# A two-phase encoder layer: the second phase turns its operands through memory and on VectorE, with three tiles in flight

## The reference

```python
h = rmsnorm(x, norm_g) * (1 + scale) + shift
rq, rk, rv, rg, aq, ak, av, ag = split(h @ w_in)           # 3328 columns
r_out = head_norm(retention(rope(rq), rope(rk), rv)) * silu(rg)    # 4 heads of 128
a_out = softmax_with_sink(aq @ ak.T / 8, window) @ av * silu(ag)   # 8 query heads, 2 key heads of 64
y = concat([r_out, a_out]) @ w_out
x = x + gate * y;   out = rmsnorm(x, final_g)
```

## Time and profile before

| what | value |
|---|---|
| median of 3 runs | 1991.48 us (1989.26 to 1991.83) |
| the profiled execution | 1995.48 us, span 1993.7 us |
| TensorE busy | 1938.5 us (97%), clock 0.989 of full |
| VectorE, ScalarE, GpSimd busy | 1089.7, 634.3, 150.9 us |
| second phase, 927 to 1993.7 us | TensorE busy 1041.31 us, VectorE 563.41, ScalarE 405.92, transfers 90 GB/s |

### The profile page before, as it was taken

The page is one execution under the profiler, slowest core; times in us unless marked ns, Lnnn a source line. Parts: engine busy times, 40 slices in busy tenths (PEclk is TensorE's granted clock), DMA queues, the critical chain, the costliest instruction groups (busy, mean ns, idle before and its releaser), DMA issues.

```text
span 1993.7 us, 30575 instructions
## 1 busy us (share of the span) xinstructions
PE 1938.5 (97%) x10240; PEld 1596.4 (80%) x10240; DVE 1089.7 (55%) x2507; ACT 634.3 (32%) x1537; POOL 150.9 (8%) x340
## 2 busy tenths in 40 slices
PE   4999999999999999998899999999999999999997
PEld 2778888888888888887688888888888888888885
DVE  3645555555555555566455555545555554555554
ACT  2312222222222221233334333333434334343332
POOL 0000000000000000000000000000000000000000
PEclk8999999999999999999899999999999999999999
DMA  9654444444444444436424243332424333242431
GB/s 350 206 142 118 117 111 115 108 110 120 120 120 120 110 111 116 108 99 184 127 69 116 63 110 82 92 105 68 116 68 105 88 86 106 67 116 70 104 79 35
DMA packets 460480, 222.22 MB, mean 111 GB/s; under 512 B 405016, under 2 KB 412376, under 8 KB 459424
## 3 DMA queue, kind: packets, MB, share of 16 engines
q1 hardware_dynamic: 460448, 221.81, 40.8%
HBM read 137.33 MB, written 84.42 MB: 111 GB/s over the span
## 4 chain that ended last, share of the span: by engine, by line
PE 91%; issue 3%; DMA 2%; DVE 2%; SPq 1%; ACT 0%; POOL 0%; POOLq 0%; DVEq 0%; ACTq 0%
PE bank L1140 74%; PE bank L1331 3%; PE bank L1314 3%; PE bank L1302 2%; PE bank L1303 2%; PE bank L1272 1%; PE bank L1213 1%; PE bank L1214 1%; PE bank L1218 1%; DMA fin_g<-in_final_g 1%; PE bank L1390 1%; PE bank L1261 1%; DMA xn_scratch<-xn 1%; SPq L386 0%; PE bank L1415 0%
## 5 line engine op out<-in xcount | busy, mean ns | idle before, releaser
L1140 PE MATMUL bank<-wh,hh 128*128 128x512 f32 x1584 | 407.3, 399 | 7.6 <-ACT wh L311 4.4
L1140 PE MATMUL bank<-wl,hh 128*128 128x512 f32 x1584 | 397.4, 393 | 0.0
L1140 PE MATMUL bank<-wh,hl 128*128 128x512 f32 x1584 | 397.2, 393 | 0.0
L1140 PEld LDWEIGHTS bank<-wl,hh 128*128 128x128 f32 x1584 | 294.9, 188 | 74.0 <-issue 12.3
L1140 PEld LDWEIGHTS bank<-wh,hl 128*128 128x128 f32 x1584 | 295.7, 188 | 62.0
L1140 PEld LDWEIGHTS bank<-wh,hh 128*128 128x128 f32 x1584 | 291.2, 190 | 65.9 <-ACT wh L311 4.7
L646 ACT ACTIVATE hf<-xn,tiny_a 128x128 f32<-128x128 f32 (+1 forms) x248 | 98.6, 480 | 383.3 <-DVE xn L817 383.3
L709 ACT ACTIVATE s_row<-s_row,tiny_b 128x256 f32<-128x256 f32 x264 | 131.1, 498 | 151.0 <-DVE tiny_b L1001 151.0
L1140 PE MATMUL bank<-wh,yh 128*128 128x512 f32 x528 | 149.7, 405 | 2.2 <-DVE yl L1085 2.2
L1140 PE MATMUL bank<-wh,yl 128*128 128x512 f32 x528 | 146.1, 399 | 0.0
L1140 PE MATMUL bank<-wl,yh 128*128 128x512 f32 x528 | 143.5, 394 | 0.0
(11 more groups left out here) (151 smaller groups left out, 2532.2 us busy)
## 6 DMA issues: line engine op xcount, KB each, us to landing
xt<-in_x_prompt SPq DMA_DIRECT2D x64, 512.0 KB, 3.9
h_scratch<-hf SPq DMA_DIRECT2D x33, 512.0 KB, 2.9
hf<-h_scratch SPq DMA_DIRECT2D x33, 512.0 KB, 4.5
out<-xt SPq DMA_DIRECT2D x32, 512.0 KB, 2.9
xn_scratch<-xn SPq DMA_DIRECT2D x31, 512.0 KB, 2.9
xp<-xn_scratch SPq DMA_DIRECT2D x124, 128.0 KB, 3.5
aq_scratch<-aq_row SPq DMA_DIRECT2D x31, 512.0 KB, 3.5
aq_row<-aq_scratch SPq DMA_DIRECT2D x124, 128.0 KB, 3.6
```

What stands on the lines that cost most here:

```text
L1140: ins = mm(out, a[:, k, :], b[:, k, :], start=first and n == part[0] and k == chunks[0], stop=last and n == part[-1] and k == chunks[-1])
```

## The change

TensorE transposes nothing in the second phase. What is turned goes out to DRAM with `store_blocks` (four stores, 32 partitions each), comes back with one plain load, and VectorE transposes its 32 x 32 blocks: queries and keys together (`aqk_row`, 640 wide), the probabilities of each half (`p_in`, 1024 wide), the gate (512 wide). A slot now holds the front of tile t, the middle of t - 1 (scores, softmax, weighing) and the back of t - 2 (output product, residual sum); the final norm and the store of y are those of t - 3. The scores are three passes (high x high, high x low, low x high) of heads of 64 rows, two key heads side by side on the row halves of the array, with `tile_position`. The masks, banks and semaphores follow; the copies of k on GpSimd fall away, since the two halves of `ak_h` are used in turn. Retention and attention chunks of the output product are done together. The other edits (the sample tile's cached keys, the mask table's order, tile 0) follow from these.

```diff
+            def store_blocks(dst, src, stored):
+                for i in range(4):
+                    sp.dma_start(dst.rearrange("(b r) (i n) -> r b i n", r=32, i=4)[:, :, i, :],
+                                 src[32 * i:32 * (i + 1)]).then_inc(stored, 16)
             def slot_b(i, u):            # SP
...
                     wait(sp, b_split, t + 1)
                     sp.dma_start(hf[:, :, :].rearrange("p k r -> p (k r)"), h_dram[t + 1]).then_inc(hb_loaded, 16)
+                    wait(sp, fin_done, t - 2)
+                        sp.dma_start(y_prompt[bass.ts(t - 3, P), :], xts[1 - u][:, :]).then_inc(y_stored[1 - u], 16)
+                    wait(sp, yr_turned, t - 1)
+                    load_blocks(yr_in, yr_dram[t - 1], yr_loaded)
+                    for half in range(2):
+                        wait(sp, exp_done, 2 * (t - 1) + half + 1)
+                        store_blocks(p_dram[2 * (t - 1) + half], s_row[:, half], p_stored[half])
+                    wait(sp, y_stored[1 - u], 16 * (i - 1 + u))
+                        sp.dma_start(xts[1 - u][:, :], x_prompt[bass.ts(t - 1, P), :]).then_inc(xb_loaded[1 - u], 16)
+                    wait(sp, p_stored[0], 4 * 16 * t)
+                    sp.dma_start(p_in[:, 0].rearrange("p b n -> p (b n)"), p_dram[2 * (t - 1)]).then_inc(p_loaded[0], 16)
+                    wait(sp, gate_scaled, t)
+                    store_blocks(g_dram[t - 1], a_gates[1 - u][:, :].rearrange("p (b n) -> p b n", b=4), g_stored)
+                    wait(sp, kv_done, t + 1)
+                    wait(sp, aq_done, t + 1)
+                    store_blocks(aqk_dram[t], aqk_row, aqk_stored)
+                    wait(sp, p_stored[1], 4 * 16 * t)
+                    sp.dma_start(p_in[:, 1].rearrange("p b n -> p (b n)"), p_dram[2 * (t - 1) + 1]).then_inc(p_loaded[1], 16)
+                    wait(sp, g_stored, 4 * 16 * t)
+                    sp.dma_start(a_gates[1 - u][:, :], g_dram[t - 1]).then_inc(g_loaded, 16)
+                    wait(sp, aqk_stored, 4 * 16 * (t + 1))
+                    sp.dma_start(aqk_row[:, :, :].rearrange("p b n -> p (b n)"), aqk_dram[t]).then_inc(aqk_loaded, 16)
...
             def slot_b(i, u):            # ScalarE
+                    # sums of squares of t - 3
+                    # yh[:, 4:8] <- g_t (ya)
                     softmax(*prev, 0)
+                    kv_rows_out()
                     softmax(*prev, 1)
+                        aq_rows_out()
+                    # gate: two tanh, then the high part of the next h
+                    # aq_h, ak_h <- aqk_f
...
+            def turn_p(i, u, half):      # VectorE
+                t = 2 * i + u
+                wait(dve, p_loaded[half], 16 * (t + 1))
+                V.transpose(s_row[:, half].rearrange("p b n -> p (b n)"),
+                            p_in[:, half].rearrange("p b n -> p (b n)")).then_inc(pt_done, 1)
             def slot_b(i, u):            # VectorE
+                    wait(dve, pv_ready, 2 * (t - 1))
+                    wait(dve, gate_turned, t - 1)
+                    V.tensor_tensor(ya, qv_b[:, :].rearrange("p (j i r) -> p j i r", j=4, i=4), ya, ALU.mult).then_inc(ya_done, 1)
                     mask_max(*prev, 0)
+                    mask_max(*prev, 1)
+                    # yl[:, 4:8] <- ya - yh
+                    wait(dve, frstd_done, t - 2)
+                    V.scalar_tensor_tensor(xts[1 - u][:, :], xts[1 - u][:, :], rstd, fin_g[:, :], ALU.mult, ALU.mult).then_inc(fin_done, 1)
+                    split_yr(i - 1, u)
+                    # den, rden; four operations, gate_scaled
+                    turn_p(*prev, 0)
+                    # ag: four operations, ag_done
+                    turn_p(*prev, 1)
+                    wait(dve, g_loaded, 16 * t)
+                    V.transpose(g_t[:, :, :, :].rearrange("p i j r -> p (i j r)"), a_gates[1 - u][:, :]).then_inc(gate_turned, 1)
                     split_hb(*nxt)
+                    wait(dve, aqk_loaded, 16 * (t + 1))
+                    V.transpose(aqk_f[:, :, :, :].rearrange("p i j r -> p (i j r)"),
+                                aqk_row[:, :, :].rearrange("p b n -> p (b n)")).then_inc(qk_turned, 1)
+                    wait(dve, qk_hi, t + 1)
+                    # aq_l, ak_l, qk_lo
+                    # the four output operations of t - 2
...
+            def scores(i, u):            # TensorE
+                wait(pe, qk_hi, t + 1)
+                wait(pe, qk_lo, t + 1)
+                for half in range(2):
+                    wait(pe, s_masked, 2 * (t - 1) + half + 1)
+                    for jl in range(2):
+                        for n, (q, k) in enumerate(((aq_h, ak_h), (aq_h, ak_l), (aq_l, ak_h))):
+                            for g in range(2):
+                                rows = slice(g * HD, (g + 1) * HD)
+                                last = mm(s_banks[2 * half + g][:, jl * 2 * P:(jl + 1) * 2 * P], q[rows, 2 * half + jl, :],
+                                          k[rows, :, :], start=n == 0, stop=n == 2, tile_position=(g * HD, 0))
             def slot_b(i, u):            # TensorE
+                    scores(*prev)
                     dense_kv(i, u)
+                    wait(pe, ya_done, t - 1)
+                    wait(pe, aq_done, t)
+                    dense(qv_b[:, :], hh0, hl0, group(0)).then_inc(zb_ready, 1)
+                    wait(pe, kv_done, t + 1)
+                    dense(kg_b[:, :], hh0, hl0, group(1)).then_inc(zb_ready, 1)
+                    wait(pe, yr_split, t - 1)
+                    dense(out0_b[:, :], yh, yl, group(2)).then_inc(o0_ready, 1)
+                    dense(out1_b[:, :], yh, yl, group(3)).then_inc(o1_ready, 1)
+                    weigh(*prev)         # waits for pt_done of each half
```

More of the change, by code:

```diff
@@ L477, in slot_b @@
                 front = not static(i) or t <= SAMPLE
[L478 to L502, removed]
+                mid = not static(i) or 1 <= t <= SAMPLE + 1
                 if not static(i) or 1 <= t < SAMPLE:
@@ L737, in slot_b @@
[L737 to L744 removed]
+                    rows = slice(HALF if static(i) and t == SAMPLE else 0, P)
@@ L1318, in weigh @@
[L1318 to L1333 removed]
+                if static(i) and t == 0:
+                    pe.wait_ge(b_set, 2)
@@ L1349, in retention_out_1 @@
-                def retention_out_1(part=(0, 1, 2)):
-                    wait(pe, aq_lo, t + 1 if front else t)
-                    ins = dense(zb1[:, :], yh, yl, group(3), part=part, chunks=range(4), first=part[0] == 0, last=False)
-                    if part[-1] == 2:
-                        ins.then_inc(yr_used, 1)
-                first = static(i) and t == 0
-                if front and not first:
-                    dense_kv(i, u)
-                if back:
-                    scores(*prev, 0)
-                    if not front:
-                        wait(pe, o0_read, t - 1)
-                        retention_out_0()
@@ L1364, in slot_b @@
-                if front and not first:
-                    wait(pe, o1_read, t - 1)
-                    dense(zb1[:, :], hh0, hl0, group(0)).then_inc(zb_ready, 1)
-                if back:
-                    turn_p(*prev, 0)
-                    scores(*prev, 1)
-                    if not front:
-                        wait(pe, o1_read, t - 1)
-                        retention_out_1()
-                if front and not first:
-                    wait(pe, ag_done, t)
-                    wait(pe, fsq_done, t - 1)
-                    dense(zb2[:, :], hh0, hl0, group(1), part=(0,), last=False)
@@ L1418, in slot_b @@
-                if back:
-                    if front:
-                        retention_out_1(part=(2,))
-                    wait(pe, ya_lo, t)
-                    dense(zb0[:, :], yh, yl, group(2), chunks=range(4, 8), first=False).then_inc(o0_ready, 1)
-                    dense(zb1[:, :], yh, yl, group(3), chunks=range(4, 8), first=False).then_inc(o1_ready, 1)
-            phase_tiles(pe, slot_b, SAMPLE + 1)
+                if mid and not (static(i) and t == 1):
+                    scores(*prev)
```

589 lines of the change are left out of this document (269 added, 320 removed).

## The result

The changed kernel takes 2046.7 us (median of 4 runs, 2045.2 to 2048.5) against 1991.7 us before: ratio 1.028, 95% interval 1.026 to 1.029. The profiled execution took 2048.5 us, its span 2046.4.

What follows compares the result with a forecast made beforehand. A closed loop through VectorE and SP's issuing was taken to bound the changed kernel: 7.2 + 17.0 + 4.5 + 8.7 = 37.4 us a tile. Span 1993.7 + 5 + 179 + 1 + 25 = 2203.7, time about 2200 us, range 2070 to 2290.

Steps and rivals of the forecast that it cites:

- TensorE's sum: TensorE's work per second-phase tile: 31.63 us falls to 28.7 if the scores' row halves run together, 30.2 if not.
- The loop: Second phase: closed round of VectorE, SP's issuing, p1's landing and VectorE/ScalarE work sets the period, 37.4 us a tile.
- VectorE's start: First part of a slot's round: ya, both masks, yl, final norm and yr on VectorE, 7.2 us.
- landing of p1: Load of the second half's probabilities, from issue to landing: 4.5 us, taken from h_scratch's load.
- VectorE and ScalarE after it: Work behind p1's load: turning p1, gate and q/k, splitting h, copies, low parts, four output operations: 8.7 us.
- the price of one store of a 32-row block: SP's time per block store, issue to issue: 0.78 us taken from yr and q/k loads; bounds 0.55 and 0.9.
- The rival of cheap stores: Rival, chance 0.17: block stores cost SP 0.55 us each, loop 33.8 us, time 2090 us.
- The low end of the loop's sum: Shortest period from the bounds on store price and landing: 32.2 us a tile, still above 31.63; highest 40.8.
- Start and end: Outside the 31 periods: tile 0's q/k round trip about 5 us later; end 54.7 us against 30, +25.
- Faster: SP is not the pace: Rival, chance 0.07: SP's issuing does not set the period; break-even 30.6 us a tile, about 1932 us at TensorE's bound.
- The heavy transfers: Rival, chance 0.08: landings and issues at their high ends, loop 40.8 us, time 2305 us.
- The clock's part: Two stands a slot may halve TensorE's clock; costed at nothing within 8.7 us slack. Rival, chance 0.03: 2340 us.

## Why the prediction was right in sign and wrong in size

**TensorE's sum: right.** 28.7 us was forecast for the row halves together. Where TensorE is the bound the beat is 28.29 to 28.33. Scores: 1.63 us for 1.4 forecast. The Trainium skill (TensorEngine Tiling (Array Packing), Key Properties) says that different tiles of the array can multiply in parallel. The trace agrees for row halves: two matmuls of 256 columns start every 0.12 us.

**The loop: right, all its links on the chain.** By its terms, in the slot shown: VectorE's start forecast 7.2, measured 6.95 (1206.87 to 1213.82); landing of p1 4.5, measured 5.4 there, 4.7 at the median; VectorE and ScalarE after it 8.7, measured 8.4 (1231.86 to 1240.27).

**The failed step: the price of one store of a 32-row block.** From yr's turn to p1's load 17.0 us were forecast and 12.66 measured (1213.82 to 1226.48). yr's loads kept their 3.2. The 16 stores took 8.3 us (4.22 + 2.15 + 1.95), 0.52 each, where 0.78 was taken; x took 0.47 for 0.74. That is 4.1 + 0.3 of the 4.65 us between the forecast beat of 37.4 and 32.75. I took the price from yr's loads because they have the same 32 partitions. The runs show that what they share is not what costs: in the loop, the patterns with a fourth dimension took 0.6 and those without 0.3 to 0.4. The nearest row was the plain issue, 0.34, and the bound that I built on it, 0.55, was still a little high. The other bound, 0.9, rested on the 0.70 of k's store as a price of three dimensions, which it was not. The rival of cheap stores had the right cause; at 33.8 it stopped one microsecond above the beat. The low end of the loop's sum, 32.2, took the beat in, but the range of the time did not go down to it.

**Start and end.** The second slot's ya was forecast at 988.3 us and began at 977.4: the first tile's round trip cost less than the 5 us given, and ya is not bound to where masking had stood before. From that ya to the one 31 periods later, at 1994.18, it was 1016.8 us where 31 x 37.4 + 1 = 1160.4 were forecast. The end took 52.2 us of 54.7. The account: 2203.7 - 10.9 - 143.6 - 2.5 = 2046.7 against a span of 2046.4.

**SP's share.** The Trainium skill's rule that the sequencer's time to start a transfer is usually small beside the transfer (DMA: Bandwidth & Descriptors, Issuing engines are not separate DMA queues) was one side of the rival that SP is not the pace. Row by row it holds, 0.32 against 2.2 to landing. It does not carry over to the sum: four stores of 1 KB cost 85 us over the kernel, moving four loads within the queue gave back 72, and issuing eight stores from ScalarE instead of SP 87.

**The rivals.** "Faster: SP is not the pace" fell. Its break-even of 30.6 us a tile was crossed only with changed orders (30.2 gave 1975). The heavy transfers did not come: landings rose by 0.2 at the median for p_in against the earlier trace rows. The clock's part was small and covered by TensorE's slack. Of two stretches of the scores in the changed kernel, the third number from the end is the granted clock:

```profile
1204.30:1205.80 1.50, 1.50 (x24) 1.46 (x24) 1.29 (x3) 0.33 (x1) 0.00 (x0) 1.00 0.14 55
...
1238.00:1240.00 2.00, 2.00 (x22) 2.00 (x22) 1.76 (x4) 0.72 (x2) 0.00 (x0) 0.50 0.04 16
```

The first follows a stand of 2.71 us, at 2.4 GHz; the second one of 3.42 us, at 1.2 GHz, and pairs of matmuls start 0.21 us apart instead of 0.12. From 1243.5 to 1245 the granted clock was 0.96 again. TensorE lost 2.6 us there (scores and k/v 7.20 us instead of 4.60), less than the 4.4 us by which the mean beat exceeds TensorE's own. The length of the stand alone does not tell which of the two comes: in the same trace one of 2.05 us (to 1270.74) was followed by half clock and one of 3.17 us (to 1401.92) was not. The prediction gave TensorE two stands a slot, 5 and 3.5 us; it had about one, of 2.9 us at the mean.

**What the prediction did not say:** that the loop's length was one of order. SP's queue reordered takes it under TensorE's sum, by itself (1909.6 us) or with VectorE's order (1908.9). The changed kernel in that order is 4% faster than the kernel before.

## What to carry to other kernels

When work moves from a matrix engine to round trips through memory, write down the closed loop through the queue that issues them, and price each issue by a row with the same pattern, its dimensions above all, and not merely the same partitions; where there is no such row, let the range go down to the sum's low end. Then ask of each issue in the loop whether it must stand there: what is not needed before the last load goes behind it, and a load into a buffer whose store was just issued stands last. To see which it is, give the engine in question a piece of work twice: here that cost 0.2 of 2.9 us while the loop was the pace, and all of it once TensorE was.

## What the runs showed of the hardware

- In the loop, the median issue on SP's queue took 0.32 to 0.43 us in three dimensions and 0.58 to 0.61 in four, loads and stores both; for stores in three dimensions, the number of pieces (128 or 512) and the bytes (1 KB or 128 KB) changed it by 0.06 or less. From start to start of such a store it is 0.50 us. The plain store of v, outside the loop, took 0.61 to 0.67 in all runs but for one of 0.34, unexplained.
- 182 GB/s in the loop, DMA share 0.63, left TensorE's pace whole (560.00 of 560 us busy; eight dense matmuls every 1.81 us, as in the changed kernel at 155 GB/s). Twice the traffic of before (93 GB/s in the same stretch) cost the bound engine nothing that can be seen.
- In the second phase of the changed kernel, 19 of 29 of TensorE's stands ahead of the scores (1.5 to 4.0 us) were followed by a stretch at half clock, some 6 us after the one of 3.42 us shown; the others, the one of 2.71 us among them, were not.
